# A hybrid decoder layer on one core: order of sums, gating and gate loads in the projection pairs

## The chip, the cores and the metric

The kernel runs on one core of a Trainium2 chip as one program. The metric is device time in microseconds; three runs of the kernel before took 2591.44, 2592.0 and 2592.83 us, median 2592.0.

## What is computed

One layer of a decoder with 2048 channels, for 512 prompt tokens and 8 sample tokens (520 in all), in float32:

```python
z = rmsnorm(x, g_mix_norm) @ w_in
uv, q, kvc, kvs, kvw, g_nsa, g_a, g_b = split_in(z)
o_a = spatial_gate(u, v, w_sgu, b_sgu)            # 1024 channels
o_b = nsa_block(q, ...)                           # sparse attention, 1024 channels
mix = sigmoid(g_a) * (o_a @ w_proj_gmlp) + sigmoid(g_b) * (o_b @ w_proj_nsa)
x = x + mix @ w_out
hm = rmsnorm(x, g_mlp_norm)
y = x + jnp.square(jax.nn.relu(hm @ w_up)) @ w_down
```

The change touches the two products with `w_proj_gmlp` and `w_proj_nsa` and the line that gates and adds them.

## The kernel before, in words

Activations lie transposed, channels on the partitions and 520 tokens along the row. A float32 product is made of three matmuls: each operand is split into a high part (ScalarE rounds a copy to fp32r) and a low part (VectorE takes the difference), and high x high, low x high and high x low are added in PSUM.

Weights of the middle of the program are worked off in 22 "pairs", `Pair(n)`. Their `part` is n - 14. Parts below 0 make the columns g_a and g_b. Part 0 to 3 multiply o_a by the four quarters of `w_proj_gmlp`, part 4 to 7 o_b by the quarters of `w_proj_nsa`; the text calls them pair 0 to pair 7. Each of them makes 4 x 128 output channels. The product is a Strassen-Winograd scheme: the weight block has four quadrants a11, a12, a21, a22 (in `w_raw`, 128 x 1024 each, 512 KB), and seven products, numbered 0 to 6, stand for eight. Their weights are, in this order: a11, a12, st_sum, the summed a21, the summed a11, the summed st_sum (the "wide sum"), a22. A product is 24 matmuls.

What each queue does for a pair, in program order (`st_pair` of each engine):

- SP loads the four quadrants of the next pair, each when the part that read its place is split (line 908).
- VectorE: `ring_in(p, k)` makes the low part of product k's weights (L2748). `st_sums(p, 0)` adds a21 to a11 (L2757), `st_sums(p, 1)` makes st_sum = a22 + a11 (L2761). `st_added` adds PSUM results to the half-made output (L2776). `gate(p, t_)` multiplies half an output by its sigmoid gates (L2837), `merge(p, t_)` adds the o_a half to the o_b half (L2843), `b_lo_in` makes the low part of the finished mix (L2659). Products 0 and 1 of a pair are prepared at the end of the pair before.
- ScalarE: its own `ring_in` makes the high parts (L1903), `st_copy` and `st_c21` copy PSUM (L1917, L1923), `b_hi_in` makes the mix's high part (L1828).
- GpSimd: `low_sum(p)` adds a22 to a21 by an accumulating DMA (L3486), `wide_sum(p)` adds a12 to st_sum in the same manner (L3491), `load_gates(p)` fetches the gate tile of a pair, 1040 KB, from DRAM (L3496). `gate_half` finishes a gate row and stores it. All wait in one queue.
- TensorE: `mix_product(p, b)` (L1399). Product k waits for the low part of its weights (`ff_lo`), product 3 also for the first `st_added` (`ff_read`), products 2, 4, 5, 6 for copies.

Every engine takes its instructions strictly in the order written. Gate tiles come into two buffers, `g_in[0]` and `g_in[1]`, used in turn. In `st_pair` of VectorE the old pair's `gate(old, 0)` and `merge(old, 0)` stand first, then `st_sums(p, 1)`.

## Time and profile before

| | us |
|---|---|
| median of three runs | 2592.0 |
| the profiled execution | 2593.7 |
| its span, first to last instruction | 2592.2 |
| TensorE matmuls busy | 2567.7 |
| VectorE busy | 2019.8 |
| ScalarE busy | 1449.5 |
| GpSimd busy | 474.0 |

The span is cut by the profile into engines' busy time; "idle before" names who ended a wait. The pairs 0 to 7 lie between 927 and 1106 us of the span, with the output projection and the feed-forward part behind them. The matmul instructions of neighbouring rows overlap (each lasts 0.28 us and one starts every 0.12 us), so the length of a stretch is read from starts, not from sums.

### The profile page before, as it was taken

The page shows a single profiled execution, that of the slowest core. Times are in us where ns is not written, and L with a number is a line of the kernel's source. Part 1 is how long each engine was busy: PE and PEld are TensorE (multiplying, and loading weights), DVE is VectorE, ACT ScalarE, POOL GpSimd, SP SyncE. Part 2 cuts the span into 40 slices and gives each one's busy share as a digit, 9 for nine tenths or more (in the row PEclk, how much of TensorE's full clock was granted, in tenths as well). Part 3 has the DMA queues.
Part 4 walks back from the last instruction along what each step waited for, and adds up shares of the span by engine and source line. Part 5 has one row for each costly group of instructions (what it writes and reads, how often), then busy time and mean ns, then how long its engine had stood idle before and what let it go on. Part 6 is the DMA issues. An engine that isn't in the chain of part 4 may idle for free. (4 is left out here: it accounts for less than half of the span.)

```text
span 2592.2 us, 56699 instructions
## 1 busy us (share of the span) xinstructions
PE 2567.7 (99%) x21295; PEld 2537.9 (98%) x21295; DVE 2019.8 (78%) x2903; ACT 1449.5 (56%) x2441; POOL 474.0 (18%) x641
## 2 busy tenths in 40 slices
PE   9999999999999999899999999999999999999998
PEld 9999999999999999899999999999999999999998
DVE  6456646668777788865688888888898888898888
ACT  6445436556444455532366656666566665666656
POOL 2001350001122221023202122121121211212113
PEclk9999999999999999999999999999999999999999
DMA  6633552214344467644336575665766756657568
GB/s 212 203 115 115 163 176 74 67 50 132 119 141 138 147 196 214 172 138 137 122 119 158 149 176 149 168 165 144 171 152 165 173 141 166 157 160 177 140 170 180
DMA packets 128089, 389.45 MB, mean 150 GB/s; under 512 B 14450, under 2 KB 16114, under 8 KB 127696
## 3 DMA queue, kind: packets, MB, share of 16 engines
q1 hardware_dynamic: 69328, 245.36, 28.1%
q0 software_dynamic: 55456, 136.73, 25.0%
q10 hardware_dynamic: 3168, 5.45, 0.6%
q8 instruction: 95, 1.56, 0.3%
q14 instruction: 42, 0.34, 0.0%
HBM read 302.77 MB, written 91.00 MB: 152 GB/s over the span
## 5 line engine op out<-in xcount | busy, mean ns | idle before, releaser
L3011 DVE TENSOR_TENSOR w_lo<-w_raw,w_hi 128x1024 fp32r<-128x1024 f32 x351 | 428.1, 1222 | 105.1 <-ACT w_hi L2027 104.2
L2027 ACT ACTIVATE w_hi<-w_raw 128x1024 fp32r<-128x1024 f32 x352 | 370.9, 1062 | 200.9 <-PE aux L1450 69.2
L1450 PE MATMUL aux<-at_t,w_hi 128*128 128x260 f32 x2016 | 368.4, 282 | 0.6 <-DVE w_lo L3011 0.5
L2204 DVE TENSOR_TENSOR w_lo<-w_raw,w_hi 128x512 fp32r<-128x512 f32 x216 | 158.9, 738 | 256.7 <-ACT w_hi L1595 255.9
L1514 PE MATMUL aux<-fb_mid,w_hi 128*128 128x260 f32 x1920 | 352.5, 284 | 1.4 <-DVE w_lo L3011 1.0
L1595 ACT ACTIVATE w_hi<-w_raw 128x512 fp32r<-128x512 f32 x216 | 135.3, 628 | 315.9 <-PE mm L1006 294.4
L1450 PEld LDWEIGHTS aux<-at_t,w_hi 128*128 128x128 f32 x2016 | 310.3, 188 | 1.3 <-DVE w_lo L3011 1.2
L1514 PEld LDWEIGHTS aux<-fb_mid,w_hi 128*128 128x128 f32 x1920 | 294.9, 188 | 2.7 <-DVE w_lo L3011 1.2
L1450 PE MATMUL aux<-at_t,w_lo 128*128 128x260 f32 x1008 | 284.2, 282 | 0.0
L1514 PE MATMUL aux<-fb_mid,w_lo 128*128 128x260 f32 x960 | 270.5, 282 | 0.0
L1514 PE MATMUL mm<-fb_mid,w_hi 128*128 128x260 f32 x1440 | 264.0, 282 | 0.0
L1006 PE MATMUL mm<-a_hi,w_hi 128*128 128x260 f32 x1216 | 254.4, 290 | 0.0
L1006 PE MATMUL mm<-a_hi,w_lo 128*128 128x260 f32 x1216 | 244.7, 283 | 0.0
L1006 PE MATMUL mm<-a_lo,w_hi 128*128 128x260 f32 x1216 | 244.2, 282 | 0.0
L1514 PEld LDWEIGHTS mm<-fb_mid,w_hi 128*128 128x128 f32 x1440 | 222.1, 188 | 0.0
L3578 POOL TENSOR_TENSOR cell<-cell 128x1 f32<-128x1 f32 x62 | 20.9, 337 | 1056.8 <-ACT y_mid L2080 1044.4
L1450 PE MATMUL mm<-at_t,w_hi 128*128 128x260 f32 x1120 | 204.8, 282 | 0.5 <-ACT hid L2063 0.5
L1514 PE MATMUL mm<-fb_mid,w_lo 128*128 128x260 f32 x720 | 203.4, 283 | 0.0
L1006 PEld LDWEIGHTS mm<-a_hi,w_hi 128*128 128x128 f32 x1216 | 187.8, 189 | 5.6 <-issue 3.8
L1450 PEld LDWEIGHTS aux<-at_t,w_lo 128*128 128x128 f32 x1008 | 189.5, 188 | 0.0
L1006 PEld LDWEIGHTS mm<-a_lo,w_hi 128*128 128x128 f32 x1216 | 187.3, 188 | 0.0
L1006 PEld LDWEIGHTS mm<-a_hi,w_lo 128*128 128x128 f32 x1216 | 187.2, 188 | 0.0
(598 smaller groups left out, 6834.2 us busy)
## 6 DMA issues: line engine op xcount, KB each, us to landing
w_raw<-in_w_ff SPq DMA_DIRECT2D x256, 512.0 KB, 3.6
out_y_t<-y_mid POOLq DMA_DIRECT2D x120, 520.0 KB, 8.0
w_raw<-in_w SPq DMA_DIRECT2D x110, 512.0 KB, 3.6
w_raw<-in_w_st SPq DMA_DIRECT2D x88, 512.0 KB, 5.0
g_in<-merge_d POOLq DMA_DIRECT2D x8, 1040.0 KB, 9.4
w_raw<-in_w_st POOLq DMA_DIRECT2D x10, 512.0 KB, 5.3
st_sum<-in_w_st POOLq DMA_DIRECT2D x10, 512.0 KB, 5.4
merge_d<-z POOLq DMA_DIRECT2D x18, 260.0 KB, 3.7
```

The lines of the kernel that those rows point to most:

```text
L1006: last = pe.matmul(mm[:, 2 * v + h, 0:HT], w, a[:, kt, h * HT:(h + 1) * HT], start=first and k == 0 and part == 0, stop=final and k == CK ...
L1450: last = pe.matmul(dst, w, at_of(j)[:, e:e + HT], start=FRESH[b] and j == 0 and part == 0, stop=j == KP - 1 and part == 2, skip_group_chec ...
L1514: last = pe.matmul(dst, w, fb[:, j, e:e + HT], start=FRESH[b] and j == 0 and part == 0, stop=j == 1 and part == 2, skip_group_check=not FR ...
L1595: run(w_hi[:, c, :], raw(u, c), ACT.Copy).then_inc(hi_split, 1)
L2027: run(hi_of(p, k), source(p, k), ACT.Copy).then_inc(ff_hi, 1)
L2204: dve.tensor_tensor(w_lo[:, c, :], raw(u, c), w_hi[:, c, :].bitcast(F32), ALU.subtract).then_inc(lo_split, 1)
L3011: dve.tensor_tensor(lo_of(p, k), source(p, k), hi_of(p, k).bitcast(F32), ALU.subtract).then_inc(ff_lo, 1)
L3578: pool.tensor_tensor(cell[:, 2:3], cell[:, 0:1], cell[:, 1:2], ALU.mult).then_inc(cell_step, 1)
```

## The change

In VectorE's `st_pair`, `st_sums(p, 1)` is written ahead of the steps for the special operands and the gating of older pairs. For pairs 5 to 7, `merge(old, 0)`, `gate(old, 1)`, `merge(old, 1)` and the two `b_lo_in` each move one or more steps back, and ScalarE's `b_hi_in` with them. GpSimd issues every gate tile load at the end of its work for a pair, behind `low_sum(to)`. The tile of pair 4 gets a place of its own, `g_late`, and is fetched during pair 3.

```diff
--- before.py
+++ after.py
@@ -476,6 +476,7 @@
         mix_home = [i1 + g_size, r1 + q_size, zone, zone + q_size]
         mix_a = [at(f"mix_a{q}", [P, 4, TOK], mix_home[q]) for q in range(4)]
         g_in = [at("g_in0", [P, 4, TOK], i1), at("g_in1", [P, 4, TOK], r1)]
+        g_late = at("g_late", [P, 4, TOK], o1 + q_size)
         late_hi = at("late_hi", [P, 2, CW], mix_home[0], F32R)
         late_lo = at("late_lo", [P, 2, CW], mix_home[0] + 8 * CW, F32R)
         nsa_t = at("nsa_t", [P, 2, NP - 1, 4, HT], i2, F32R)
@@ -757,7 +758,10 @@
             return x[:, 4 * p.q + t_:4 * p.q + 4:2, :]
 
         def gate_part(p, t_):
-            return g_in[p.part % 2][:, t_:4:2, :]
+            return gates_home(p)[:, t_:4:2, :]
+
+        def gates_home(p):
+            return g_late if p.part == N_PROJ // 2 else g_in[p.part % 2]
 
         def at_of(j):
             return at_last[:, :] if type(j) is int and j == KP - 1 else at_t[:, j, :]
@@ -1951,9 +1955,9 @@
                     gm_hi(B22)
                 if p.part in (1, 2):
                     nsa_hi(B11, js)
+                ring_in(p, 4)
                 if p.part > 4:
                     b_hi_in(old, 0)
-                ring_in(p, 4)
                 if not old:
                     gate_out(2 * M_ST - 1)
                 if p.part == -1:
@@ -1964,8 +1968,6 @@
                     nsa_hi(B21, js)
                 if p.part == 3:
                     nsa_hi(T2)
-                if p.part > 4:
-                    b_hi_in(old, 1)
                 if old and p.part < 0:
                     st_tanh(old, 0)
                 st_copy(p, 1)
@@ -1978,6 +1980,8 @@
                     nsa_hi(T3)
                 st_copy(p, 2)
                 ring_in(p, 6)
+                if p.part > 4:
+                    b_hi_in(old, 1)
                 if p.part == -1:
                     gm_hi(T2)
                 if p.part == 0:
@@ -2846,21 +2850,20 @@
                 old = Pair(p.n - 1) if p.n else None
                 older = Pair(p.n - 2) if p.n > 1 else None
                 js = slice(2 * p.part - 2, 2 * p.part)
-                if p.part == 0:
-                    gm_lo(T2)
-                if p.part == 1:
-                    nsa_t2()
-                if p.part == 4:
-                    gate(older, 0)
-                if p.part > 4:
-                    gate(old, 0)
-                    merge(old, 0)
                 if old:
                     st_sums(p, 1)
                     if not p.loaded_sums:
                         st_sums(p, 2)
                     if p.part == -1:
                         st_scale(old, 0)
+                    if p.part == 0:
+                        gm_lo(T2)
+                    if p.part == 1:
+                        nsa_t2()
+                    if p.part == 4:
+                        gate(older, 0)
+                    if p.part > 4:
+                        gate(old, 0)
                     ring_in(p, 2)
                     if p.part < -1:
                         st_scale(old, 0)
@@ -2875,8 +2878,7 @@
                     if p.part == 4:
                         gate(older, 1)
                     if p.part > 4:
-                        gate(old, 1)
-                        merge(old, 1)
+                        merge(old, 0)
                     ring_in(p, 3)
                 if not p.loaded_sums:
                     st_sums(p, 3)
@@ -2906,8 +2908,8 @@
                 if p.part == 4:
                     gate(old, 0)
                 if p.part > 4:
-                    b_lo_in(old, 0)
-                    b_lo_in(old, 1)
+                    gate(old, 1)
+                    merge(old, 1)
                 if old and p.part < -1:
                     st_scale(old, 1)
                 elif not old:
@@ -2924,7 +2926,11 @@
                     nsa_lo(KP + NP + 10, T3)
                 if p.part == 4:
                     gate(old, 1)
+                if p.part > 4:
+                    b_lo_in(old, 0)
                 ring_in(p, 6)
+                if p.part > 4:
+                    b_lo_in(old, 1)
                 if p.part == -1:
                     gm_t3()
                 if p.part == 0:
@@ -3493,7 +3499,7 @@
             def load_gates(p):
                 for t_ in range(2):
                     pool.wait_ge(g_stored[t_], 64 * (p.q + 1))
-                pool.dma_start(g_in[p.part % 2][:, :, :], merge_d.rearrange("(q k t) p n -> t q p k n", k=4, t=2)[
+                pool.dma_start(gates_home(p)[:, :, :], merge_d.rearrange("(q k t) p n -> t q p k n", k=4, t=2)[
                     p.phase][p.q]).then_inc(g_loaded[p.part % 2], 16)
 
             for n in range(N_SUMMED - 2):
@@ -3504,33 +3510,28 @@
                 p, old, to = Pair(n), Pair(n - 1), Pair(n + 1)
                 if p.loaded_sums:
                     wide_sum(p)
+                if p.part <= 0:
+                    gate_half(M_ST + n - 1, 0, st_out(old, 0))
                 if p.part < 0:
-                    gate_half(M_ST + n - 1, 0, st_out(old, 0))
+                    gate_half(M_ST + n - 1, 1, st_out(old, 1))
+                if p.part < N_PROJ - 1:
+                    low_sum(to)
                 if p.part == 0:
+                    gate_half(M_ST + n - 1, 1, st_out(old, 1))
                     pool.wait_ge(ff_used, old.used + NP)
                     load_gates(p)
-                if p.part == 4:
-                    pool.wait_ge(gated, KP + 6)
+                if p.part == 1:
+                    pool.wait_ge(mix_lo, GM_DONE)
                     load_gates(p)
-                if p.part > 4 and p.part < N_PROJ - 1:
-                    pool.wait_ge(gated, KP + 2 * p.part)
-                    load_gates(to)
-                if p.part < 0:
-                    gate_half(M_ST + n - 1, 1, st_out(old, 1))
-                if p.part == 0:
-                    pool.wait_ge(mix_lo, GM_DONE)
-                    load_gates(to)
-                    gate_half(MB - 1, 0, st_out(old, 0))
                 if p.part in (2, 3):
                     pool.wait_ge(gated, KP + 2 * p.part - 2)
                     load_gates(p)
-                if p.part == 4:
-                    pool.wait_ge(gated, KP + 8)
+                if p.part == 3:
+                    pool.wait_ge(ff_used, p.used + NP)
                     load_gates(to)
-                if p.part < N_PROJ - 1:
-                    low_sum(to)
-                if p.part == 0:
-                    gate_half(MB - 1, 1, st_out(old, 1))
+                if p.part in (4, 5, 6):
+                    pool.wait_ge(gated, KP + (8, 6, 12)[p.part - 4])
+                    load_gates(to)
             pool.wait_ge(b_ready, N_PROJ)
             steps.did(pool.memset(acc_x[:, :], 0.0))
```

VectorE from the end of pair 5 to the third product of pair 6, before. `w_raw<-w_raw` is `st_sums(p, 0)`, `late_lo` is the low part for product 1 and `st_sum<-w_raw` is `st_sums(p, 1)`.

```order
L2757 TENSOR_TENSOR w_raw<-w_raw 128x1024 [waits ff_lo,ff_loaded2]
L2776 TENSOR_TENSOR b_f<-b_f,aux 128x2x260 [waits ff_used,ff_copied]
L2748 TENSOR_TENSOR late_lo<-w_raw,late_hi 128x1024 [waits ff_hi]
L2837 TENSOR_TENSOR b_f<-b_f,g_in_161 128x2x520 [waits ff_read,g_loaded1]
L2843 TENSOR_TENSOR b_f<-b_f,mix_a_157 128x2x520 [waits xs_scaled]
L2761 TENSOR_TENSOR st_sum<-w_raw 128x1024 [waits ff_sum,ff_loaded3]
L2748 TENSOR_TENSOR w_lo<-st_sum,w_hi 128x1024 [waits ff_hi]
L2837 TENSOR_TENSOR b_f<-b_f,g_in_161 128x2x520 [waits ff_c21,ff_read,g_loaded1]
```

The same place in the changed kernel:

```order
L2761 TENSOR_TENSOR w_raw<-w_raw 128x1024 [waits ff_lo,ff_loaded2]
L2780 TENSOR_TENSOR b_f<-b_f,aux 128x2x260 [waits ff_used,ff_copied]
L2752 TENSOR_TENSOR late_lo<-w_raw,late_hi 128x1024 [waits ff_hi]
L2765 TENSOR_TENSOR st_sum<-w_raw 128x1024 [waits ff_sum,ff_loaded3]
L2841 TENSOR_TENSOR b_f<-b_f,g_in_161 128x2x520 [waits ff_read,g_loaded1]
L2752 TENSOR_TENSOR w_lo<-st_sum,w_hi 128x1024 [waits ff_hi]
L2847 TENSOR_TENSOR b_f<-b_f,mix_a_157 128x2x520 [waits xs_scaled]
L2752 TENSOR_TENSOR w_lo<-w_raw,w_hi 128x1024 [waits ff_hi]
L2780 TENSOR_TENSOR b_f<-b_f,mm 128x2x260 [waits ff_used,ff_copied]
L2752 TENSOR_TENSOR late_lo<-w_raw,late_hi 128x1024 [waits ff_hi]
```

st_sum has moved from behind gate and merge to directly behind product 1's low part; gate now stands between it and its low part, merge ahead of product 3's low part, and the second gate behind product 4's. (Line numbers of the changed file are 4 higher here.)

GpSimd from the wide sum of pair 3 to that of pair 5, before. `w_raw<-in_w_st` is a low sum, `st_sum<-in_w_st` a wide sum.

```order
L3491 DMA st_sum<-in_w_st 128x1024 [waits ff_lo]
L3496 DMA g_in_161<-merge_d 128x4x520 [waits g_stored1,g_stored0,xs_scaled]
L3486 DMA w_raw<-in_w_st 128x1024 [waits ff_sum]
L3491 DMA st_sum<-in_w_st 128x1024 [waits ff_lo]
L3496 DMA g_in_160<-merge_d 128x4x520 [waits g_stored1,g_stored0,xs_scaled]
L3496 DMA g_in_161<-merge_d 128x4x520 [waits g_stored1,g_stored0,xs_scaled]
L3486 DMA w_raw<-in_w_st 128x1024 [waits ff_sum]
L3491 DMA st_sum<-in_w_st 128x1024 [waits ff_lo]
```

The same place in the changed kernel:

```order
L3497 DMA st_sum<-in_w_st 128x1024 [waits ff_lo]
L3492 DMA w_raw<-in_w_st 128x1024 [waits ff_sum]
L3502 DMA g_in_161<-merge_d 128x4x520 [waits g_stored1,g_stored0,xs_scaled]
L3502 DMA g_late<-merge_d 128x4x520 [waits g_stored1,g_stored0,ff_used]
L3497 DMA st_sum<-in_w_st 128x1024 [waits ff_lo]
L3492 DMA w_raw<-in_w_st 128x1024 [waits ff_sum]
L3502 DMA g_in_161<-merge_d 128x4x520 [waits g_stored1,g_stored0,xs_scaled]
L3497 DMA st_sum<-in_w_st 128x1024 [waits ff_lo]
```

Both gate tiles that are now issued between pair 4's low sum and its wide sum (those of pairs 3 and 4) stood outside that stretch before; from pair 5 on a tile stands between each low sum and wide sum.

GpSimd behind the wide sum of pair 0, before, to the low sum of pair 1:

```order
L3491 DMA st_sum<-in_w_st 128x1024 [waits ff_lo]
L3496 DMA g_in_160<-merge_d 128x4x520 [waits g_stored1,g_stored0,ff_used]
L3496 DMA g_in_161<-merge_d 128x4x520 [waits g_stored1,g_stored0,st_ready]
L632 TENSOR_TENSOR small<-ones 128x1 [waits g_tanh]
L3453 TENSOR_SCALAR z<-z 128x520
L3456 DMA merge_d<-z 128x520 [waits g_stored0,pool_step]
L3486 DMA w_raw<-in_w_st 128x1024 [waits ff_sum]
```

The same place in the changed kernel, to the wide sum of pair 1:

```order
L3497 DMA st_sum<-in_w_st 128x1024 [waits ff_lo]
L633 TENSOR_TENSOR small<-ones 128x1 [waits g_tanh]
L3459 TENSOR_SCALAR z<-z 128x520
L3462 DMA merge_d<-z 128x520 [waits g_stored0,pool_step]
L3492 DMA w_raw<-in_w_st 128x1024 [waits ff_sum]
L633 TENSOR_TENSOR small<-ones 128x1 [waits g_tanh]
L3459 TENSOR_SCALAR z<-z 128x520
L3462 DMA merge_d<-z 128x520 [waits g_stored1,pool_step]
L3502 DMA g_in_160<-merge_d 128x4x520 [waits g_stored1,g_stored0,ff_used]
L3497 DMA st_sum<-in_w_st 128x1024 [waits ff_lo]
```

The two tiles that stood directly behind pair 0's wide sum are gone from there. One of them is now behind the last gate row's store, the other one pair later.

## Rows read from the trace of the kernel before

**Rows 1.** The page, section 1: busy time of each engine.

```profile
PE 2567.7 (99%) x21295; PEld 2537.9 (98%) x21295; DVE 2019.8 (78%) x2903; ACT 1449.5 (56%) x2441; POOL 474.0 (18%) x641
```

**Rows 2.** Waits of TensorE: total us, times, longest us.

```profile
PE aux L1399 <- DVE a_lo L2748: 3.8, 2, 2.0
PE aux L1399 <- DVE w_lo L2748: 3.1, 2, 2.2
PE aux L1399 <- DVE b_f L2776: 2.3, 2, 1.1
...
PE mm L1399 <- ACT mix_a L1917: 0.4, 1, 0.4
```

**Rows 3.** Stretches of pairs 0, 1, 2, 6, 7; the first line names the columns.

```profile
core 0: us, PE busy (x) PEld busy (x) DVE busy (x) ACT busy (x) POOL busy (x), PEclk, DMA share, GB/s
927.80:948.70 20.90, 20.45 (x170) 20.10 (x168) 17.05 (x17) 11.43 (x15) 5.46 (x7) 1.00 0.80 229
950.50:956.00 5.50, 5.50 (x33) 5.50 (x34) 5.43 (x5) 0.64 (x2) 2.68 (x4) 0.69 0.51 89
950.50:973.70 23.20, 22.33 (x170) 22.00 (x171) 21.36 (x22) 11.79 (x17) 4.23 (x6) 0.93 0.58 154
973.70:993.80 20.10, 20.10 (x171) 20.10 (x170) 17.89 (x19) 12.05 (x16) 2.65 (x4) 1.00 0.77 210
1057.76:1081.57 23.81, 20.52 (x170) 20.13 (x169) 19.38 (x19) 11.81 (x14) 2.46 (x3) 1.00 0.64 178
1081.57:1105.66 24.09, 20.73 (x171) 20.34 (x170) 21.35 (x22) 11.98 (x16) 1.71 (x2) 1.00 0.58 153
```

**Rows 4.** Timeline of VectorE in pair 6: start, us, instruction.

```profile
1059.75 1.23 DVE L2837 TENSOR_TENSOR b_f<-b_f,g_in 128x1040 f32<-128x1040 f32 x1
...
1062.18 1.22 DVE L2761 TENSOR_TENSOR st_sum<-w_raw 128x1024 f32<-128x1024 f32 x1
1064.52 1.22 DVE L2748 TENSOR_TENSOR w_lo<-st_sum,w_hi 128x1024 fp32r<-128x1024 f32 x1 [1.12 <-ACT w_hi L1903]
```

**Rows 5.** Timeline of TensorE, its restarts in pairs 1 and 6.

```profile
950.48 0.39 PE L1399 MATMUL aux<-a_hi 128*128 128x260 f32 x1 [1.75 <-DVE a_lo L2748]
...
1065.80 0.51 PE L1399 MATMUL mm<-nsa_t,w_hi 128*128 128x260 f32 x2 [2.15 <-DVE w_lo L2748]
1070.06 0.49 PE L1399 MATMUL mm<-nsa_t,w_hi 128*128 128x260 f32 x2 [1.14 <-DVE b_f L2776]
```

**Rows 6.** Timeline of ScalarE, boundary of pairs 0 and 1, and pair 6.

```profile
948.11 1.06 ACT L1903 ACTIVATE a_hi<-w_raw 128x1024 fp32r<-128x1024 f32 x1 [3.29 <-DMA w_raw<-in_w_st]
...
1063.43 1.06 ACT L1903 ACTIVATE w_hi<-st_sum 128x1024 fp32r<-128x1024 f32 x1 [4.87 <-DVE st_sum L2761]
...
1071.46 1.06 ACT L1903 ACTIVATE w_hi<-st_sum 128x1024 fp32r<-128x1024 f32 x1 [1.69 <-DMA st_sum<-in_w_st]
```

**Rows 7.** Timeline of GpSimd, pairs 0, 4 and 6.

```profile
934.65 1.13 POOL L3496 DMA_DIRECT2D g_in<-merge_d  x1
943.34 0.80 POOL L3496 DMA_DIRECT2D g_in<-merge_d  x1 [7.56 <-DVE a_lo L2647]
...
1012.73 0.84 POOL L3486 DMA_DIRECT2D w_raw<-in_w_st  x1 [6.84 <-DVE w_raw L2757]
...
1058.38 0.83 POOL L3486 DMA_DIRECT2D w_raw<-in_w_st  x1 [14.33 <-DVE w_raw L2757]
1066.04 0.85 POOL L3491 DMA_DIRECT2D st_sum<-in_w_st  x1 [6.83 <-DVE w_lo L2748]
1067.19 0.79 POOL L3496 DMA_DIRECT2D g_in<-merge_d  x1 [0.31 <-DVE b_f L2837]
```

**Rows 8.** Line 3496, the eight gate tile loads.

```profile
DMA to landing us min/median/max: 5.8/9.4/13.0
```

**Rows 9.** Line 3491, the eight wide sums.

```profile
DMA to landing us min/median/max: 5.0/5.4/5.5
```

**Rows 10.** A stretch at full DMA rate, columns as in rows 3.

```profile
1007.90:1011.10 3.20, 3.20 (x29) 3.20 (x29) 3.20 (x4) 1.56 (x3) 0.00 (x0) 1.00 1.00 400
```

## Prediction

> **What bounds the kernel now.** The page comes first: TensorE is busy for 99% of the span [rows 1], so only its idle time, or time at a lower granted clock, can be won. Next I read who TensorE waits for. Nearly all of what can be won is at line 1399, the projection pairs 0 to 7; [rows 2] has four of the six kinds of wait. Third come the stretches from one pair's first matmul to the next one's [rows 3]. A pair without waits takes 20.10 us (pairs 2, 3 and 4 all do). Pair 0 takes 20.9, pair 1 takes 23.2, pair 6 takes 23.81 (pair 5 the same) and pair 7 takes 24.09. Between pairs 0 and 1 TensorE stood for 1.75 us [rows 5]. Everything above 20.1 adds up to 0.8 + 1.8 + 3.1 + 3.7 + 3.7 + 4.0 = 17.1 us, and no reordering in this stage can win more.
>
> Where this comes from is read in pair 6, counted from its first matmul at 1057.76 and written as +t. Its seven products take 2.87 us each, so products 0 and 1 end at +5.7. Product 2 needs the sum st_sum (one VectorE step), its high part (ScalarE, 1.06) and its low part (VectorE, 1.22). VectorE finishes the low part of product 1 at +2.0, then gates and merges half a tile of the old pair, and starts st_sum only at +4.4; ScalarE starts on it at +5.7, VectorE's low part at +6.8 [rows 4, 6], and TensorE has stood for 2.15 us [rows 5]. The same lateness returns at product 3, which waits 1.14 us for the first addition of the results. Pairs 5 and 7 repeat this.
>
> At the boundary of pairs 0 and 1 the cause is another: ScalarE idles 3.29 us for the DMA of the first weight block [rows 6], while GpSimd had put two gate tiles of 1040 KB into flight at 934.65 and 943.34 [rows 7]. After the 1.75 us pause the granted clock was 0.69 over the next 5.5 us [rows 3], that is partly the lower of the two levels.
>
> **The change, part by part.**
>
> *st_sum ahead of gate and merge, pairs 5 to 7.* It starts at +2.0 instead of +4.4. High part from +3.3 to +4.3; one gate step of 1.15 fits beside it; low part +4.4 to +5.6. Product 2 can start at +5.7, just on time: the 2.15 goes. What is late next is product 3's operand: the summed block, whose accumulating DMA is issued at +0.6 [rows 7] and lands, taken as its sister's 5.4 [rows 9], at about +5.9. High part to +7.0, low part to +8.2, addition to +8.8, against a due time of +8.6: 0.2 us of wait stays where 1.14 was. The one merge that now stands before product 3's low part ends at +6.7, so ScalarE's wait hides it.
>
> Then VectorE itself. A pair has 15 steps of 1.15 and 3 of 0.61, 19.1 us, and it cannot avoid small waits for ScalarE (0.1, 0.3, 0.3, some at the next first block). So a pair takes 19.8 to 20.8 us by VectorE and 20.1 by TensorE. Following both halves of b_lo around product 6, the next pair's product 1 gets its low part at +1.6 to +2.4 of that pair, not +2.0 for certain; each tenth beyond that is a tenth of TensorE's wait. I take 20.8 per pair. The three go from 71.7 to 62.4 us: **9.3 won**, bounds 6.5 (21.75 per pair) and 11.4 (20.1). ScalarE's b_hi moved behind part 4 and part 6 costs nothing: it was busy 11.8 of 23.8 us [rows 3] and VectorE's half that needs it stands later too.
>
> *The same move in pairs 0, 1 and 4.* In pair 0 the high part is 1.15 us earlier, so the copy for which product 2 waited 0.4 is earlier too [rows 2]: 0.4 won. In pair 1 nsa_t2 goes behind st_sum, and 0.9 of wait (the second of the w_lo waits in [rows 2]) falls to about 0.3. Pair 4 had no wait there: 0. What is moved back, gm_lo, nsa_t2 and the gating of pair 2, is needed by products or pairs later than the ones they precede; 1.15 us late costs them nothing.
>
> *Gate tiles issued behind the next pair's sum.* From 934 to 950 no gate tile is in flight, the first one leaves near 952, behind the block sum of pair 1 and the last gate store. The weight block that came in 9 us then comes in 5 to 6, ahead of its use: the 1.75 goes (1.8 with its restart), and with it the lower clock, which I price as pair 1's 23.2 less 20.1 less the 0.9 wait: 2.2. Bounds: 0 if another transfer holds the block, 4.0.
>
> The cost is on GpSimd's queue. Now the wide sum (the accumulating DMA for product 5) leaves at +8.3 with the gate tile behind it [rows 7] and lands 5.4 later, hardly ever otherwise [rows 9]. After the change every pair from 1 to 7 has low sum (+0.6), gate tile (+1.7), wide sum (+5.9) in one queue. No row shows an accumulate behind a gate tile. Bounds: alone it would land at +11.3; if it starts only once a gate tile has landed after the median 9.4 [rows 8], +11.1, plus its own 3.2 of data, at +14.3. Product 5 starts at +14.4 to +14.6 and needs high and low part (2.4) before that, so it is due at +12.0 to +12.2. Data rates say where between: full-speed stretches move 400 GB/s [rows 10], so a gate tile is 2.7 us of data and a weight block 1.3. Behind the low sum's end (+5.7) that gives +9.7, and the wide sum would land at +12.9 if all of a12's block shares the time, +11.6 if none. I take +12.2: no stall of its own, but VectorE's later steps slip with it, which is why I took 20.8 and not 20.3 above. In pair 1 the tile leaves only 2.5 us ahead of the wide sum: I take a 0.5 stall (0 to 2.3). Pairs 2 and 3 have 2 to 3 us of slack, 0.
>
> *Pair 4 has two tiles* (g_in and g_late) behind its low sum of 1012.73 [rows 7], 1.2 before the pair's start. Data: low sum to 1017.8 (5.1 after issue, [rows 9]), two tiles and a block 6.7, so 1024.5, wide sum to 1027.7, parts to 1030.1. Product 5 is due at 1013.9 + 14.4 = 1028.3. VectorE's low part would end 1.8 late; the block takes only part of its share ahead of the sum, so I take **1.5 lost**. Bounds: 0.5 if the block comes wholly behind, 4 if both tiles hold the queue as in the upper bound.
>
> The Trainium skill, DMA: Bandwidth & Descriptors, section Queues, rings and completion order, says that descriptors of one queue are taken in ring order and that an engine alternates between queues by packet. That speaks against the change: the wide sum cannot overtake a gate tile. Its fit for a GpSimd DMA in the same page's section Anatomy of one DMA (2.0 us plus bytes at 436 GB/s, an estimate here) gives 4.4 us for a gate tile where [rows 8] has 5.8 at the least and 9.4 in the middle; by it the wide sums would not be late at all and the sum would be about 2576.
>
> *Sum.* 0.4 + 1.8 + (2.2 + 0.6 - 0.5) + 9.3 - 1.5 = 12.3 us. The profiled execution took 2593.7 us (span 2592.2), 1.7 above the median of 2592.0; taken from it this leaves 2581.4, and against the median **2579.7 us**. Behind pair 7 the output projection and the feed-forward part have TensorE without waits worth naming, so a gain reaches the end; the tail of pair 7 keeps its order on VectorE, and b_lo has about 2 us of slack there.
>
> **Rivals.** A measurement of this kernel can tell about 0.2% (5 us) from no change.
>
> *Gate tiles free of cost.* The wide sums land as before and VectorE keeps up: late pairs at 20.3, pairs 1 and 4 without stall: 0.4 + 1.8 + 2.8 + 10.8 = 15.8, 2576. For it: the 400 GB/s. Against: the 9.4 median. 0.16.
>
> *Boundary stays.* The first weight block of pair 1 is late for another reason, so 1.8 and 2.2 remain: 8.3 won, 2583.7. Against it: two megabytes leave exactly that stretch. 0.14.
>
> *The wide sum takes the place.* It lands at the upper bound, +14.3: product 5 starts 2.3 late in pairs 5 to 7 (23.1 each, 2.4 won), pair 1 loses 2.3, pairs 2 and 3 together 1, pair 4 loses 4: 0.4 + 1.8 + 2.8 + 2.4 - 7.3 = 0.1, 2592. For it: the 9.4 and 13.0 landings [rows 8]; against: those were measured beside two weight blocks. 0.12.
>
> *Slower: these waits lower the clock.* With the wide sum at the upper bound, waits of 2.3 and 4 us stand in pairs 1, 4, 5, 6 and 7. If each is followed by the lower level as the 1.75 us pause was, at 2.2 each, 11 are added: 2603. It decides from a landing of about +13.5 on. Against it: the waits of 2.15 in pairs 5 to 7 left the granted clock at 1.00 [rows 3]. 0.07.
>
> **How the numbers follow.** Forecast 0.51. The forecast's own range is 2576.5 to 2583; 8 in 10 must reach past the boundary case and part of the way to the fourth: 2575.5 to 2588. Faster: 0.51 + 0.16 + 0.14 = 0.81. Same: 0.12. Slower: 0.07.
>
> **What would show it.** Pairs 5 to 7 at 20.3 to 21.3 us each; TensorE's w_lo waits of about 2.1 gone, the b_f ones at 0 to 0.4; ScalarE's wait for st_sum's DMA longer than 1.69; no pause and no clock below 1.00 between pairs 0 and 1; a new wait at product 5 of pair 4. The forecast is wrong if a late pair takes over 22 us, if pair 4 loses over 3, or if the clock drops behind a new wait.

## The result, and the profile after

The changed kernel takes 2603.48 us (median of 6 runs, 2599.31 to 2606.61), the kernel before 2592.08 (2591.4 to 2593.72). The ratio is 1.0044, with a 95% interval from 1.0032 to 1.0055: slower by 11.4 us, where 12.3 us faster had been forecast. Its six runs spread over 7.3 us, the six of before over 2.3; but 26 further runs of the kernel before (2589.52 to 2595.84) spread over 6.3, so that it is less steady is not shown.

First the stretches of the eight pairs in the changed kernel, the counterpart of [rows 3], with the same columns:

```profile
core 0: us, PE busy (x) PEld busy (x) DVE busy (x) ACT busy (x) POOL busy (x), PEclk, DMA share, GB/s
928.70:948.80 20.10, 20.10 (x170) 20.10 (x170) 19.28 (x20) 13.61 (x17) 5.68 (x6) 1.00 0.62 161
948.80:973.00 24.20, 21.91 (x171) 21.70 (x170) 20.29 (x22) 11.87 (x16) 5.62 (x8) 0.93 0.65 194
973.00:993.70 20.70, 20.47 (x171) 20.26 (x170) 15.87 (x17) 12.11 (x16) 1.04 (x3) 1.00 0.71 204
993.70:1017.00 23.30, 20.40 (x170) 20.21 (x170) 17.50 (x17) 12.64 (x15) 2.43 (x3) 1.00 0.65 182
1017.00:1046.80 29.80, 23.23 (x169) 22.75 (x168) 19.84 (x20) 9.77 (x12) 4.97 (x6) 0.89 0.63 184
1046.80:1066.90 20.10, 20.10 (x170) 20.10 (x169) 17.24 (x16) 11.73 (x14) 0.84 (x1) 1.00 0.67 203
1066.90:1094.40 27.50, 23.24 (x170) 22.95 (x169) 21.64 (x22) 11.68 (x14) 4.10 (x5) 0.88 0.57 156
1094.40:1118.30 23.90, 21.98 (x171) 21.77 (x170) 18.37 (x19) 11.99 (x16) 0.87 (x1) 0.93 0.67 188
```

Pairs 0 and 5 take the 20.1 us of a pair without waits. Pair 0 is 0.8 shorter than before, and the pause between pairs 0 and 1 is gone. But pair 1 takes 24.2, pair 3 takes 23.3 (20.1 before), pair 4 takes 29.8 (20.1 before), pair 6 takes 27.5 and pair 7 takes 23.9. What stands above 20.1 is 28.8 us, against 17.1 before.

Who TensorE waits for there, the counterpart of [rows 2] (total us, times, longest us):

```profile
PE mm L1403 <- DVE w_lo L2752: 10.5, 2, 6.3
PE aux L1403 <- DVE w_lo L2752: 4.2, 2, 2.3
PE aux L1403 <- ACT mix_a L1921: 2.9, 1, 2.9
...
PE mm L1403 <- DVE b_f L2780: 0.3, 1, 0.3
```

The three waits of 2.0 to 2.2 us ahead of product 2 are gone and the waits for b_f, up to 1.1 us, are down to a single one of 0.3. In their place stand five long waits ahead of product 5, up to 6.3 us, in pairs 1, 3, 4, 6 and 7. The one put down to ScalarE's copy mix_a is pair 3's: the copy stood in ScalarE's order behind the high part of the wide sum, which had waited 5.37 us for the DMA (the line at 1008.47 further down). VectorE's timeline in pair 6 (start, us), the counterpart of [rows 4], shows both at once:

```profile
1067.56 1.22 DVE L2752 TENSOR_TENSOR late_lo<-w_raw,late_hi 128x1024 fp32r<-128x1024 f32 x1
1068.70 1.22 DVE L2765 TENSOR_TENSOR st_sum<-w_raw 128x1024 f32<-128x1024 f32 x1
1069.83 1.24 DVE L2841 TENSOR_TENSOR b_f<-b_f,g_in 128x1040 f32<-128x1040 f32 x1
1071.05 1.22 DVE L2752 TENSOR_TENSOR w_lo<-st_sum,w_hi 128x1024 fp32r<-128x1024 f32 x1
...
1084.54 1.23 DVE L2752 TENSOR_TENSOR w_lo<-st_sum,w_hi 128x1024 fp32r<-128x1024 f32 x1 [5.53 <-ACT w_hi L1907]
```

Pair 6 starts at 1066.9. st_sum starts at +1.8, where it had been +4.4, and product 2's low part at +4.2: the reordering does what it was written for. Further down, product 5's low part starts at +17.6, after VectorE had stood for 5.53 us. The hold-up is one step earlier, on ScalarE, whose bracket names a DMA (counterpart of [rows 6]; pairs 3, 4 and 6):

```profile
1008.47 1.06 ACT L1907 ACTIVATE w_hi<-st_sum 128x1024 fp32r<-128x1024 f32 x1 [5.37 <-DMA st_sum<-in_w_st]
...
1036.01 1.06 ACT L1907 ACTIVATE w_hi<-st_sum 128x1024 fp32r<-128x1024 f32 x1 [9.56 <-DMA st_sum<-in_w_st]
...
1083.46 1.06 ACT L1907 ACTIVATE w_hi<-st_sum 128x1024 fp32r<-128x1024 f32 x1 [7.12 <-DMA st_sum<-in_w_st]
```

And that DMA is the wide sum, on GpSimd's queue (counterpart of [rows 7]; pair 4 from its first tile, then pair 6):

```profile
1018.74 0.79 POOL L3502 DMA_DIRECT2D g_in<-merge_d  x1 [0.20 <-issue]
1019.51 0.80 POOL L3502 DMA_DIRECT2D g_late<-merge_d  x1
1022.94 0.91 POOL L3497 DMA_DIRECT2D st_sum<-in_w_st  x1 [2.62 <-DVE w_lo L2752]
...
1067.34 0.84 POOL L3492 DMA_DIRECT2D w_raw<-in_w_st  x1 [16.35 <-DVE w_raw L2761]
1067.89 1.07 POOL L3502 DMA_DIRECT2D g_in<-merge_d  x1
1072.57 0.85 POOL L3497 DMA_DIRECT2D st_sum<-in_w_st  x1 [3.61 <-DVE w_lo L2752]
```

In pair 6 the wide sum is issued at 1072.57 and its reader starts at 1083.46, 10.9 us later. In pair 4, behind two tiles, it is 1022.94 to 1036.01, 13.1 us. Over the ten DMAs of this line (the wide sums of pairs 0 to 7 and two of the stage ahead of them):

```profile
DMA to landing us min/median/max: 5.4/8.5/13.1
```

against 5.0/5.4/5.5 in [rows 9]. That line, too, has these ten, and not the eight that its heading says. The eight gate tiles:

```profile
DMA to landing us min/median/max: 8.4/10.2/12.7
```

The tile of pair 6 is issued at 1067.89 and lands after 12.0 us, at 1079.9; the wide sum lands 3.6 us after it. In pair 4 g_late lands 12.7 us after 1019.51, at 1032.2, and the wide sum 3.8 us after that. A wide sum alone needs 5.4 us from issue; here it moved behind the tile. The two can be told apart in the trace, because a packet of the tile has 4160 bytes and one of the sum 4096. In pair 6 the sum's first packet moves at 1076.8, 4.2 us after the issue, when 87% of the tile's packets have moved; in pairs 2 to 7 it is 87 to 97% before the sum has its first. The 16 DMA engines do not end together, though: 234 of the tile's 256 packets in pair 6 had moved by 1077.3, the last moved at 1079.2, and the engines that had done their share went on with the sum.

Why the tile itself takes 12.0 us is read from pair 6 cut at the wide sum's issue (the low sum lands at the same time, 1072.5), and at the tile's landing, same columns:

```profile
1067.90:1072.50 4.60, 4.60 (x41) 4.60 (x40) 4.60 (x5) 1.55 (x2) 1.06 (x2) 1.00 0.71 145
1072.50:1079.90 7.40, 7.40 (x63) 7.31 (x62) 6.29 (x6) 3.58 (x4) 0.85 (x1) 1.00 0.99 273
```

The low sum ahead of the tile takes the first 4.6 us. Then, for 7.4 us, the DMA engines are full (0.99) but move 273 GB/s, 2.0 MB in all. By queue (packets, MB, share of the engines' time; q0 is GpSimd's, q1 SP's):

```profile
q0 software_dynamic: 348, 1.37, 70.9%
q1 hardware_dynamic: 172, 0.64, 27.1%
```

GpSimd's 1.37 MB are 0.92 of the tile, which has 1.06 in all, and 0.44 of the wide sum; SP's 0.64 are a little more than one weight block of 0.52. From the tile's landing to 1083.5 GpSimd's queue moves only 0.08 MB more and SP's 0.88. So in pair 6 the sum lands 3.6 us after the tile because its last engines come late to it, not because most of its bytes were still to move; in pairs 2 and 3 some 90 of its 128 packets moved after the tile's landing.

Last the clock. The stretches behind the five waits of 1.9 us and more, same columns:

```profile
965.60:970.00 4.40, 4.40 (x23) 4.40 (x24) 4.17 (x6) 2.61 (x4) 0.00 (x0) 0.61 0.33 107
1011.10:1017.00 5.90, 5.88 (x49) 5.90 (x50) 5.78 (x6) 4.28 (x5) 0.00 (x0) 1.00 0.24 89
1038.40:1046.40 8.00, 8.00 (x45) 8.00 (x46) 7.14 (x8) 2.61 (x4) 1.64 (x2) 0.64 0.31 81
1085.80:1092.00 6.20, 6.17 (x28) 6.18 (x29) 6.10 (x6) 3.06 (x5) 0.00 (x0) 0.50 0.24 85
1110.90:1118.00 7.10, 7.10 (x46) 7.10 (x47) 7.00 (x8) 3.75 (x7) 0.00 (x0) 0.76 0.33 103
```

A granted clock of 0.50 is the lower of the two levels (1.2 GHz and 2.4 GHz), 1.00 the upper, and the other figures are mixtures. Behind four of the five waits (2.29, 6.27, 4.26 and 1.92 us) the level fell; behind the 2.90 us wait of pair 3 it did not. Pair lengths less 20.1 less their waits give 1.8, 3.1, 3.1 and 1.9 us for these four, 9.9 us in all. Most of that is the clock; pair 3, whose clock stayed, has 0.3 beyond its wait, so about 0.3 of each is the restart itself.

### The profile page after: what moved, and what is told of

Same layout as the page of the kernel before. It is cut to its first block and busy times, and to the rows that moved or that the text cites. A ratio compares the mean times of both kernels' runs of the same rounds, so it can differ in the third digit from the quotient of the medians.

```text
span 2603.8 us, 56700 instructions
## 1 busy us (share of the span) xinstructions
PE 2573.6 (99%) x21295; PEld 2544.3 (98%) x21295; DVE 2019.4 (78%) x2903; ACT 1448.5 (56%) x2441; POOL 479.1 (18%) x641
## 5 line engine op out<-in xcount | busy, mean ns | idle before, releaser
L3579 POOL TENSOR_TENSOR cell<-cell 128x1 f32<-128x1 f32 x62 | 20.8, 335 | 1054.0 <-ACT y_mid L2084 1042.1
```

The lines of the kernel that those rows point to most:

```text
L3579: pool.tensor_tensor(cell[:, 2:3], cell[:, 0:1], cell[:, 1:2], ALU.mult).then_inc(cell_step, 1)
```

## The experiments

Seven kernels were run. Each is an edit of the changed kernel or of the one before.

### 1. VectorE's and ScalarE's order alone

```diff
 # the changed kernel, GpSimd's block for the pairs put back to that of before
-        g_late = at("g_late", [P, 4, TOK], o1 + q_size)
-            return g_late if p.part == N_PROJ // 2 else g_in[p.part % 2]
+            return g_in[p.part % 2]
```

> VectorE's and ScalarE's new order with GpSimd's queue as in the kernel before, g_late left out. Theory Q (the loss comes from gate tiles ahead of the wide sums in one queue): the wide sums land 5.4 us after issue, late pairs take 20.8 us or less, about 9 us faster than before: 2583 (2580 to 2586); the pause and the lower clock between pairs 0 and 1 stay. Theory V (the new order on VectorE is itself at fault, its steps slip behind TensorE): pairs 5 to 7 stay at 23.8 or more and the time is 2592 or above.

Measured: 2580.03 us against 2592.82, ratio 0.9947 (0.9933 to 0.996). Pairs 5, 6 and 7, and the stretch behind the boundary of pairs 0 and 1:

```profile
1032.60:1052.70 20.10, 20.10 (x170) 20.10 (x169) 18.14 (x18) 11.70 (x14) 1.68 (x3) 1.00 0.75 213
1052.70:1073.10 20.40, 20.39 (x170) 20.20 (x170) 19.79 (x20) 11.81 (x14) 2.51 (x4) 1.00 0.75 207
1073.10:1093.90 20.80, 20.38 (x170) 20.20 (x169) 19.45 (x20) 11.99 (x16) 1.66 (x2) 1.00 0.63 160
950.40:956.00 5.60, 5.60 (x45) 5.47 (x46) 5.59 (x5) 1.49 (x3) 2.68 (x4) 1.00 0.51 98
```

The three late pairs take 61.3 us, where they took 71.7. VectorE in pair 6, which starts at 1052.7:

```profile
1054.43 1.22 DVE L2764 TENSOR_TENSOR st_sum<-w_raw 128x1024 f32<-128x1024 f32 x1
...
1056.78 1.23 DVE L2751 TENSOR_TENSOR w_lo<-st_sum,w_hi 128x1024 fp32r<-128x1024 f32 x1
```

The order is that of the changed kernel and so are the starts: st_sum at +1.7, product 2's low part at +4.1. The wide sums:

```profile
DMA to landing us min/median/max: 5.3/5.5/5.8
```

So the reordering on VectorE and ScalarE wins 12.8 us by itself, somewhat more than the 9.3 + 0.4 + 0.6 given to it, and everything that the changed kernel loses comes from GpSimd's half: 2603.5 less 2580.0, 23.5 us, and this although that half removes the pause at the boundary. In the trace 10.4 us of the gain lie in pairs 5 to 7 and 2.5 in pairs 0 and 1. The latter are not all the edit's: in this execution the pause at the boundary was 1.06 us instead of 1.75 and the clock behind it stayed at 1.00, while pair 1's wait ahead of product 2 stayed (1.01 us; 0.3 had been forecast). Theory V is refuted.

### 2. GpSimd's order alone

```diff
 # the kernel before, with the changed kernel's GpSimd block
+        g_late = at("g_late", [P, 4, TOK], o1 + q_size)
+            return g_late if p.part == N_PROJ // 2 else g_in[p.part % 2]
```

> GpSimd's new order and g_late with VectorE's and ScalarE's order of before. Theory Q: wide sums land 8 to 13 us after issue in pairs 1 to 4 and TensorE waits there as in the changed kernel (2.3, 0.2, 2.9, 6.3, each long one followed by the lower clock); in pairs 5 to 7 the wide sum is issued some 2.4 us later than in the changed kernel and product 5 is due later too, so 23.8 to 25 us each; sum 2600 to 2606. Theory V: no slower than before, 2588 to 2592, since the boundary's 4 us are won.

Measured: 2600.72 us, ratio 1.0029 (1.002 to 1.0039). TensorE's two longest waits and the wide sums' landing:

```profile
988.88 0.59 PE L1403 MATMUL mm<-a_hi 128*128 128x260 f32 x1 [3.39 <-DVE a_lo L2752]
...
1038.06 0.80 PE L1403 MATMUL mm<-nsa_t,w_hi 128*128 128x260 f32 x2 [4.07 <-DVE w_lo L2752]
```

```profile
DMA to landing us min/median/max: 5.4/6.7/11.2
```

The two are ahead of product 5 in pairs 2 and 4, and the lower clock follows both. Product 5 of pairs 1 and 3, for which 2.3 and 2.9 had been expected, does not wait here; pair 1's 1.5 stands ahead of product 2. Pairs 5 to 7 take 21.6, 22.1 and 22.1 us, not the 23.8 to 25 expected: the 1.1 at product 3 is left, but product 2 waits only 0.4. That was a miss. VectorE is earlier there: it begins with the old pair's gate 0.2 us after the start of pair 6, where it had been 2.0, and ScalarE's wait of 1.67 us for a weight block at the end of pair 5 is gone. That this is so because no tile stands in the way of the weight loads late in the pair is argued and not tested. The main point of theory Q holds: GpSimd's order alone is slower than before, although it removes the pause at the boundary.

### 3. Each tile directly behind a wide sum

```diff
 # the changed kernel; in GpSimd's loop, directly behind wide_sum(p):
+                if p.part == 1:
+                    pool.wait_ge(ff_used, Pair(N_ST - 1).used + NP)
+                    load_gates(old)
+                if p.part == 2:
+                    pool.wait_ge(mix_lo, GM_DONE)
+                    load_gates(old)
+                if p.part == 3:
+                    for q in (old, p):
+                        pool.wait_ge(gated, KP + 2 * q.part - 2)
+                        load_gates(q)
+                if p.part == 4:
+                    pool.wait_ge(ff_used, old.used + NP)
+                    load_gates(p)
+                if p.part > 4:
+                    pool.wait_ge(gated, KP + (8, 6, 12)[p.part - 5])
+                    load_gates(p)
 # and none behind low_sum(to)
```

> The changed kernel with each gate tile issued directly behind a wide sum, none between a low sum and the next wide sum (tile 0 behind wide sum 1, tile 1 behind 2, tiles 2 and 3 behind 3, g_late behind 4, then each pair's own). Theory Q: wide sums land in 5.4 us, no wait over 0.5 us and no lower clock in pairs 0 to 6, late pairs 20.3 to 20.8: 2578 to 2582, faster than both kernels. Theory B (the DMA engines are full whatever the order, the tiles displace weight loads instead): waits return at the first product of a pair for its weight block; 2588 or more.

Measured: 2586.76 us, ratio 0.9979 (0.997 to 0.9988). The wide sums land in 5.3 to 6.3 us and no wait of TensorE is over 0.4, as theory Q has it. But the list of TensorE's idle times has twelve small ones, 3.7 us together, and pairs 2 to 7 take 21.3 to 22.0 us. (Each such restart costs some 0.2 us more than the wait listed, and pauses under 0.15 us are not listed.) The gain is half of what was expected. The likely reason is theory B's. ScalarE's waits for weight blocks, here:

```profile
ACT w_hi L1907 <- DMA w_raw<-in_w_st: 16.0, 11, 2.9
...
ACT a_hi L1907 <- DMA w_raw<-in_w_st: 5.3, 4, 2.5
```

and in experiment 1:

```profile
ACT a_hi L1906 <- DMA w_raw<-in_w_st: 4.7, 4, 3.0
ACT w_hi L1906 <- DMA w_raw<-in_w_st: 4.6, 7, 1.2
```

With late_hi (4.2 and 2.0 us) these are 25.5 us of such waits over the whole program against 11.3. A tile that leaves 0.6 to 1.0 us behind the wide sum meets SP's weight blocks, which come due in the same microseconds; in experiment 1 the tile of a late pair leaves 5.2 us or more behind the wide sum. That these waits make up the lost half is read from the two traces, not tested by an edit of its own.

### 4. The tiles on another queue

```diff
 # the changed kernel; load_gates moved from GpSimd to the end of ScalarE's pair
+                act.dma_start(gates_home(p)[:, :, :], merge_d.rearrange("(q k t) p n -> t q p k n", k=4, t=2)[
+                    p.phase][p.q]).then_inc(g_late_loaded if p.part == 4 else g_loaded[p.part % 2], 16)
```

> The changed kernel with the gate tiles issued from ScalarE's queue at the end of its pair, about when GpSimd issues them in the changed kernel; same bytes at the same time, but another queue. Theory Q (order within the queue): the wide sum no longer has to let the tile pass, it lands 5.5 to 8 us after issue instead of 8 to 13; 2580 to 2588. Theory B (bandwidth of the DMA engines): landings as in the changed kernel, 2598 or more.

Measured: 2592.8 us, ratio 1.0002 (0.9992 to 1.0011), neither theory's number; its ten runs lie between 2586.8 and 2599.2. The wide sums:

```profile
DMA to landing us min/median/max: 5.4/6.9/7.4
```

They land in 7.4 us at most where it was 13.1. But the tiles did not move at the same time as in the changed kernel: ScalarE issued seven of the eight 1.4 to 3.2 us ahead of the low sum, not behind it, and those had landed before the wide sum was issued. Only g_late, in pair 4, was in flight when a wide sum left: issued at 1017.69, landed at 1029.4, with the sum issued at 1022.87. That sum landed after 7.4 us, 0.9 behind the tile, where behind two tiles in its own queue it had needed 13.1. This one pair speaks for the queue; the other six do not separate the theories. The low sums, which had been ahead of the tile, now share the DMA engines with it and take longer:

```profile
DMA to landing us min/median/max: 5.3/7.8/8.8
```

(5.0/5.4/5.5 in the changed kernel.) TensorE's waits moved with it, from product 5 to product 3, where the low sum is needed:

```profile
PE aux L1404 <- DVE mix_a L2798: 3.5, 2, 2.5
PE aux L1404 <- DVE b_f L2798: 3.0, 2, 2.1
```

So both are true. The place in the queue decides who is delayed, and the bytes cost too: the low sums beside a tile took 6.8 to 8.8 us, 1.4 to 3.3 more than in the changed kernel. In every pair the wide sum was issued 1.5 to 3.6 us before this late low sum had landed, which is a likely reason for its own 6.8 to 7.4 us in six of the seven.

### 5. The good order, with the early tiles moved

```diff
 # experiment 1; in GpSimd's loop
-                if p.part == 0:
-                    pool.wait_ge(ff_used, old.used + NP)
-                    load_gates(p)
+                if p.part == 1:
+                    pool.wait_ge(ff_used, Pair(N_ST - 1).used + NP)
+                    load_gates(old)
 ...
+                if p.part == 1:
+                    pool.wait_ge(mix_lo, GM_DONE)
+                    pool.wait_ge(ff_lo, p.e + 6)
+                    load_gates(p)
```

> e1_order_alone with the two gate tiles of pair 0 moved: tile 0 behind wide sum 1, tile 1 once pair 1's low part 5 is made; all others as in e1. Theory Q: from 934 to 950 no tile is in flight, the 1.06 us pause and the lower clock between pairs 0 and 1 go, and since no tile stands between a low sum and a wide sum nothing else waits: 3 to 4 us below e1, 2576 to 2577. Theory B (tiles cost wherever they are put, as small waits in e3 suggest): pairs 1 or 2 lengthen by what the boundary gives, 2579 to 2581.

Measured: 2578.88 us, ratio 0.9945 (0.9931 to 0.9959). Pair 0 takes 20.1 us; the stretch behind the boundary:

```profile
948.90:956.00 7.10, 7.10 (x61) 7.07 (x60) 7.02 (x7) 4.05 (x6) 3.82 (x6) 1.00 0.81 215
```

The pause and the lower clock are gone, as expected. The whole from the start of pair 0 to the end of pair 7 is 0.6 us shorter than in experiment 1, because pairs 2 and 5 take 21.6 and 21.4 us here, where they took 20.1. The median lies next to theory B's range (2579 to 2581) and not in theory Q's (2576 to 2577), though the interval reaches both; as theory B has it, what the boundary gave came back as small waits in other pairs. The two kernels' intervals overlap: it is faster than both kernels of this case, but not shown to be faster than experiment 1.

### 6. Only st_sum moved, nothing spread

```diff
 # experiment 1, VectorE
                         gate(old, 0)
+                        merge(old, 0)
                     ring_in(p, 2)
 ...
-                        merge(old, 0)
+                        gate(old, 1)
+                        merge(old, 1)
                     ring_in(p, 3)
 # b_hi_in and b_lo_in as in the kernel before
```

> Of the new order only the first part: st_sum ahead of the old pair's gate and merge, which stay together behind it, second gate and merge ahead of product 3, b_hi and b_lo where they were in the kernel before; GpSimd as before. If the spreading matters: product 2 waits for the merge that stands before its low part (1.1 instead of 2.1) and product 3 about 1.3, late pairs 22.5, about 2587. If st_sum's place alone is what counts: as e1, 2580.

Measured: 2586.19 us, ratio 0.9977 (0.9967 to 0.9986); 2587 was expected. TensorE's restarts in pair 6:

```profile
1060.68 0.51 PE L1402 MATMUL mm<-nsa_t,w_hi 128*128 128x260 f32 x2 [1.11 <-DVE w_lo L2751]
1064.93 0.48 PE L1402 MATMUL mm<-nsa_t,w_hi 128*128 128x260 f32 x2 [1.10 <-DVE b_f L2779]
```

1.11 us at product 2, as worked out, and 1.10 at product 3. Pairs 5 to 7 take 22.3, 22.9 and 22.7 us. So in these three pairs st_sum's place alone wins 3.8 us of the 10.4 of experiment 1, and the spreading behind it the rest. In this execution there was no pause between pairs 0 and 1, although GpSimd's order is that of before; the pause varies from one execution to the next (1.75, 1.06 and none with this order), so the difference of the medians, 5.7 us of 12.8, flatters st_sum's place.

### 7. Pair 4 with one tile in the way instead of two

```diff
 # the changed kernel, GpSimd's loop: g_late's load behind wide_sum(4)
-                if p.part == 3:
-                    pool.wait_ge(ff_used, p.used + NP)
-                    load_gates(to)
+                if p.part == 4:
+                    pool.wait_ge(ff_used, old.used + NP)
+                    load_gates(p)
```

> The changed kernel with only g_late's load moved, from behind pair 3's tile to behind wide sum 4. Theory Q: pair 4's wide sum, landing 13.1 us after issue behind two tiles, lands in 9 to 10 behind one; its 6.3 us wait falls to 2 to 3 and the lower clock behind it shrinks; 5 to 7 us below the changed kernel, 2596 to 2599. Theory B: the bytes are the same, at most 1 us, 2602 or more.

Measured: 2599.76 us, ratio to before 1.0029 (1.0019 to 1.0039), 3.7 below the changed kernel; 2596 to 2599 had been expected. Product 5 of pair 4:

```profile
1035.80 0.51 PE L1403 MATMUL mm<-nsa_t,w_hi 128*128 128x260 f32 x2 [1.08 <-DVE w_lo L2752]
```

Its wide sum lands 8.8 us after issue, the wait is 1.08 instead of 6.27 and pair 4 takes 21.5 us instead of 29.8. That is more than expected for the pair, less for the whole. Pair 5 goes from 20.1 to 25.4: in the changed kernel its low sum had left 2.8 us before the pair's start, VectorE having got ahead in the slow pair 4, and here it leaves 0.2 before, so the wide sum lands at +15.7 and not at +11.4. Pairs 6 and 7 are 5.5 us shorter together. Pair 3 is 2.2 us longer, but its late wide sum (10.2 us) was issued before anything that the edit moves: single pairs vary by this much from one execution to the next, and only the median of the eight runs is a result.

## Why the prediction was wrong

**The step that failed is the cost on GpSimd's queue.** The prediction put a wide sum that leaves 4 us behind a gate tile at a landing of +12.2, from data rates: 2.7 us for the tile at 400 GB/s, 3.2 for the sum. The trace shows +16.6 in pair 6 (1083.46 less 1066.90) and +19.0 in pair 4 (1036.01 less 1017.00). Two sizes were off. The tile, given 4.0 us behind the low sum with a weight block beside it (+9.7 less +5.7), needed 7.4 in pair 6. About nine tenths of its packets had moved after 4.8 us, but it lands with its slowest engine; meanwhile SP's blocks and the wide sum itself moved too, 273 GB/s in all, not the 400 of [rows 10]. Why some engines fell behind stays open. And the wide sum, given 2.5 behind the tile, landed 3.2 to 4.2 behind it. Chained behind the low sum's issue that is 5.2 + 7.4 + 3.6 = 16.2 us where the prediction had 11.6. Even its upper bound, +14.3, was passed in pairs 1, 3, 4 and 6 (+14.4, +14.7, +19.0 and +16.6) and nearly met in pair 7 (+14.1); only pairs 2 and 5 came near the forecast (+12.4, +11.4). The bound was too low because it put the tile at the median of [rows 8], and those tiles had no low sum right ahead of them. What the tile must wait for was left out of the bound.

**What was known of the queue.** The wide sum landed 3.2 to 4.2 us after the tile in each of the seven pairs, and with the tiles out of its way (experiments 1 and 3) it landed 5.3 to 6.3 us after its issue. The Trainium skill, DMA: Bandwidth & Descriptors, section Queues, rings and completion order, has the descriptors of a queue taken in ring order; it says so of the queues of SP and ScalarE. The traces agree for GpSimd's: the tile's packets first, then the sum's. The prediction drew the right conclusion, that the sum cannot overtake the tile, and then priced the tile at a full rate. The fit of the Trainium skill, DMA: Bandwidth & Descriptors, section Anatomy of one DMA, 2.0 us plus bytes at 436 GB/s, gives 4.4 us for a tile (an estimate). No tile here was that fast: 8.4 us is the least in the changed kernel, 5.8 before, 5.2 from ScalarE's queue.

**VectorE's part was right, mechanism and size.** Late pairs of 20.8 were forecast and experiment 1 has 20.1, 20.4 and 20.8: 10.4 us against 9.3. The wait for b_f at product 3 fell to 0.4 at most. Only pair 1's wait at product 2 was not cut to 0.3 by it (1.01 in experiment 1).

**The boundary was right.** The pause and the lower clock behind it are gone in the changed kernel and in the five experiments that move the early tiles, and pair 0 takes 20.1. But part of the 4.0 us was not sure to be there: with the tiles in their old place the pause was 1.06 in experiment 1 and absent in experiment 6.

**Pair 4** had been given 1.5 us, bounds 0.5 and 4. It lost 9.7: 6.3 of wait, 0.3 at product 3, 3.1 by the clock and the restarts. The wide sum landed at +19.0, not +13.8: the low sum was issued 0.7 after the pair's start and not 1.2 before it, its landing and the two tiles took 14.5 us and not 11.8, and the sum 3.8 and not 3.2.

**The rival that came true is the fourth.** It was named with its mechanism, its place (product 5 of pairs 1 and 4 to 7) and 2603 us, and was given 0.07, the third rival with the same queue 0.12. Two things are not as it had them. Pair 3, with 2 to 3 us of slack by the prediction, waits 2.9, and pair 5 does not wait. That its number was met to the microsecond is luck: by it pairs 5 to 7 take 75.9 us (23.1 and 2.2 for the clock, each), and they took 71.5; pair 4 loses 6.2 by it, and lost 9.7; pairs 2 and 3 lose 1, and lost 3.8. And the argument against it, that waits of 2.15 us had left the clock at 1.00, rested on three waits. In the nine traces 17 waits of TensorE in pairs 0 to 7 are 1.75 us or longer. The lower level followed 13 of them: 1.75, 1.92, 2.07, 2.18, 2.29, 2.48, 2.78 and all six from 3.39 up. It did not follow 2.04, 2.15, 2.22 and 2.90, nor any wait of 1.6 or less. No length separates the two groups, and why the 2.90 us wait kept its clock stays open.

What [rows 8 and 10] held was enough for a better bound. The 400 GB/s is a tile with the engines nearly to itself: the one issued at 1005.10 moved in that stretch and landed after 5.8 us, the least of the eight. The median of 9.4 us is of tiles beside weight blocks, which is the case here; put behind the low sum instead of behind an empty queue it gives +0.6, 5.2, some 7 to 9 us and 3.2 to 3.6 of the sum, +16 to +18 where +12.2 was due (an estimate, made with the result known). The prediction did name those blocks, but as a reason against the rival.

## What to carry to other kernels

When a large transfer is moved, ask first what is issued behind it in the same queue, and add up the data times of everything between the last idle moment of that queue and the transfer that someone waits for; the latency of one transfer in a quiet queue says nothing about it, nor does a peak rate while other queues are loading. A transfer lands when the slowest of its engines is done. A slot that frees one stretch (here the boundary of two pairs) can lie right ahead of the transfer with the least slack. A change with two independent halves is worth running as halves: here one half won 12.8 us and the other lost 23.5 on top of it.

## What the runs showed of the hardware that was not expected

- An accumulating DMA of 512 KB lands 5.0 to 5.8 us after its issue when no tile stands right ahead of it: 97 of the 100 in the traces of the kernel before and of experiments 1, 3, 5 and 6, the others in 6.0 to 6.3. Beside a 1040 KB transfer that ScalarE issued, the low sums of experiment 4 took 6.8 to 8.8.
- It uses the DMA engines at half the rate of a plain load. While the low sum of pair 6 moves (1070 to 1072 in the changed kernel) they are full (1.01 and 1.03) at 201 and 209 GB/s, against 400 in [rows 10]; one of its packets of 4096 bytes takes 0.33 us, one of a weight block 0.16.
- While it moves, SP's loads hardly do: from 936 to 940 us in the kernel before, GpSimd's queue had 94% of the engines' time and SP's 0.3%, and a weight block issued between 936 and 937 moved its first packet only at 939.8.
- The same tile lands in 5.2 to 11.7 us, median 6.4, from ScalarE's queue, most of them ahead of the low sum (the 11.7 is the one behind it), and in 8.4 to 12.7, median 10.2, from GpSimd's behind a low sum.
- A wait can be dearer than its length: 14.7 us of waits in pairs 1, 4, 6 and 7 of the changed kernel cost 9.9 us more, most of it through the granted clock.
